# Convolution mixer by token tiles instead of channel halves, and 512-token tiles in the second group's FFN projections

## The reference

```python
def swiglu(x, w_in, w_down):
    a = x @ w_in
    gate, up = jnp.split(a, 2, axis=-1)
    return (jax.nn.silu(gate) * up) @ w_down

def conformer_conv(x, buf, w_in, conv_w, conv_b, ln_g, ln_b, w_out):
    a = x @ w_in                                          # (B, L, 2D)
    glu = a[..., :D_MODEL] * jax.nn.sigmoid(a[..., D_MODEL:])
    ext = jnp.concatenate([buf.astype(glu.dtype), glu], axis=1)   # (B, 30+L, D)
    c = depthwise_conv(ext, conv_w) + conv_b
    c = jax.nn.silu(layernorm(c, ln_g, ln_b))
    return c @ w_out, ext[:, -(CONV_A_WIDTH - 1):]

for i in range(DEPTH):
    f = swiglu(rmsnorm(h, g[0]), ffn_w_in[i, 0], ffn_w_down[i, 0])
    h = h + FFN_HALF * rmsnorm(f, g[1])
    xm = rmsnorm(h, g[2])
    ...                     # mixer i: convolution, gated convolution, gMLP, pooling
    h = h + rmsnorm(m, g[3])
    f = swiglu(rmsnorm(h, g[4]), ffn_w_in[i, 1], ffn_w_down[i, 1])
    h = h + FFN_HALF * rmsnorm(f, g[5])
```

## Time and profile before

| | |
|---|---|
| median of 3 runs | 4662.27 us (4657.13 to 4664.7) |
| the profiled execution | 4654.91 us |
| its span on the slowest core | 4653.4 us |
| spans of the 8 cores | 4644.1 to 4653.4 us |
| TensorE busy | 4566.7 us, 98% |
| VectorE, ScalarE, GpSimd busy | 1770.4, 1281.3, 608.6 us |
| matmuls | 30474 |

### The profile page before, as it was taken

The page is one execution under the profiler, slowest core; times in us unless marked ns, Lnnn a source line. Parts: engine busy times, 40 slices in busy tenths (PEclk is TensorE's granted clock), DMA queues, the critical chain, the costliest instruction groups (busy, mean ns, idle before and its releaser), DMA issues.

```text
span 4653.4 us, 83035 instructions; the slowest of 8 cores (4644.1 to 4653.4 us)
## 1 busy us (share of the span) xinstructions
PE 4566.7 (98%) x30474; PEld 2698.2 (58%) x30474; DVE 1770.4 (38%) x3156; ACT 1281.3 (28%) x2499; POOL 608.6 (13%) x1102
## 2 busy tenths in 40 slices
PE   7998999999999999999999989999999999999999
PEld 4555656556555565565646566565665655656564
DVE  2366232373232542326232472323723236232622
ACT  2135222233221331224121252222322225121421
POOL 1112110011010110102010111101101012010210
PEclk9998999999999999999999999999999999999999
DMA  8336527264263543635565246363543636444361
GB/s 167 68 73 124 103 53 137 48 117 85 55 111 62 106 84 61 118 60 93 98 139 98 63 90 112 57 118 57 105 92 57 117 57 123 73 80 98 60 119 41
DMA packets 228042, 416.39 MB, mean 89 GB/s; under 512 B 114095, under 2 KB 136879, under 8 KB 227630
## 3 DMA queue, kind: packets, MB, share of 16 engines
q0 software_dynamic: 88592, 319.79, 39.6%
q1 hardware_dynamic: 139054, 91.30, 8.0%
HBM read 682.92 MB, written 12.71 MB: 149 GB/s over the span
## 4 chain that ended last, share of the span: by engine, by line
PE 92%; DVE 2%; issue 2%; DMA 2%; SPq 1%; ACT 1%; POOL 0%; DVEq 0%; ACTq 0%; POOLq 0%
PE ps L83 91%; DVE big L88 1%; SPq L242 1%; PE ps L84 1%; ACT big L85 1%; DVE big L86 1%; DMA big<-wst 1%; DMA big<-big 1%; DMA big<-xp 0%; DVE big L89 0%; POOL big L86 0%; DVE big L87 0%; DVEq L167 0%; POOL big L242 0%; ACTq L167 0%
## 5 line engine op out<-in xcount | busy, mean ns | idle before, releaser
L83 PE MATMUL ps<-big 128*128 128x384 bf16 (+5 forms) x29758 | 4535.4, 322 | 47.6 <-DMA big<-big 13.3
L83 PEld LDWEIGHTS ps<-big 128*128 128x128 bf16 (+1 forms) x29758 | 2653.9, 99 | 1897.5 <-issue 137.4
L85 ACT ACTIVATE big<-ps 128x384 f32<-128x384 f32 (+5 forms) x1526 | 875.4, 577 | 2829.1 <-PE ps L83 2721.3
L86 DVE TENSOR_TENSOR big<-ps,big 128x384 bf16<-128x384 f32 (+6 forms) x1386 | 856.6, 618 | 1855.6 <-PE ps L83 1838.0
L88 DVE SCALAR_TENSOR_TENSOR big<-big 128x1024 bf16<-128x1024 f32 (+9 forms) x591 | 585.4, 995 | 184.0 <-POOL big L86 115.8
L242 POOL DMA_DIRECT2D big<-wst x608 | 327.2, 542 | 2456.3 <-PE ps L83 2296.4
L85 ACT ACTIVATE big<-big 128x1024 bf16<-128x1024 f32 (+5 forms) x454 | 344.4, 774 | 480.8 <-DVE big L88 308.7
L86 POOL TENSOR_TENSOR big<-big 128x1 f32<-128x1 f32 (+1 forms) x434 | 261.8, 605 | 1537.7 <-DVE big L87 1313.8
L87 DVE TENSOR_SCALAR big<-big 128x1 f32<-128x1 f32 (+2 forms) x439 | 78.6, 180 | 716.7 <-ACT big L85 703.2
L89 DVE COPY big<-big 32x1136 bf16<-32x1136 bf16 (+4 forms) x281 | 81.7, 291 | 19.5 <-ACT big L85 7.8
L84 PE MATMUL ps<-big 128*128 128x128 bf16 x716 | 57.5, 224 | 29.3 <-DVE big L88 18.1
(11 more groups left out here) (9 smaller groups left out, 20.5 us busy)
## 6 DMA issues: line engine op xcount, KB each, us to landing
big<-wst POOLq DMA_DIRECT2D x608, 512.0 KB, 8.4
big<-gains SPq DMA_DIRECT2D x52, 512.0 KB, 10.6
big<-xp SPq DMA_DIRECT2D x16, 512.0 KB, 5.1
yp<-big SPq DMA_DIRECT2D x16, 512.0 KB, 4.1
big<-big SPq DMA_DIRECT2D x64, 71.0 KB, 2.5
big<-big SPq DMA_DIRECT2D x64, 70.8 KB, 2.7
big<-big SPq DMA_DIRECT2D x48, 64.0 KB, 2.3
big<-dwx SPq DMA_DIRECT2D x4, 512.0 KB, 4.3
```

The costliest lines, as they stand in the source:

```text
L83: 'matmul': lambda e, *a, **k: e.matmul(*a, **k),
L85: 'activation': lambda e, *a, **k: e.activation(*a, **k),
L86: 'tensor_tensor': lambda e, *a, **k: e.tensor_tensor(*a, **k),
```

## The change

Two things change. The convolution mixer projects all eight channel blocks of a token tile before the next token tile, and its passes go by `ct` with both halves together; the slots lent for results are four instead of six, in another order among the weights; the second group has three `xr` buffers instead of two; the DVE copies of a gather are written into DVE's order where its modelled queue is short (`polite`). And in the second group the FFN projections run over two token tiles of 512 instead of 384, 384 and 256; the staging room of 4608 bytes is three buffers of 384 or two of 512, and the class `Widths` keeps overlapping ones apart. The first group's FFNs and the other mixers keep their tiles.

```diff
+class Widths(Pool):
+    CLASH = {0: (3,), 1: (3, 4), 2: (4,), 3: (0, 1), 4: (1, 2)}
...
+    def take(self, wide):
+        c = [i for i in ((3, 4) if wide else (0, 1, 2)) if i not in self.busy and not any(x in self.busy for x in self.CLASH[i])]
+        if not c:
+            return None
+        k = min(c, key=lambda i: self.S.p.rt_w([(self.name, x) for x in (i,) + self.CLASH[i]]))
+        self.S.p.inherit([(self.name, k)], [(self.name, x) for x in self.CLASH[k]])
+        self.busy.add(k)
+        return k
...
                     for q in range(4):
                         cast(('ai', q, 0), ('in', 'a_w_in', q * 256))
                         cast(('ai', q, 1), ('in', 'a_w_in', D + q * 256))
-                        if q == 1:
-                            for i in range(4):
-                                lend(('W', i))
-                            for i in range(2):
-                                lend(('C', i))
-                            lend(('F', 0))
-                            lend(('F', 1))
-                    for i in range(2, 6):
+                    for i in range(2):
+                        lend(('W', 2 * i))
+                        lend(('W', 2 * i + 1))
+                        lend(('C', i))
+                        lend(('F', i))
+                    for i in range(2, 4):
                         lend(('F', i))
...
-        sg = [A.at(SG0 + i * 1536, [384], F32) for i in range(3)]
+        sg = [A.at(SG0 + i * 1536, [384], F32) for i in range(3)] + [A.at(SG0 + i * 2560, [512], F32) for i in range(2)]
...
+        def polite(eng='dve'):
+            while p.efree[eng] > S.now + 0.25:
+                yield p.efree[eng] - 0.15
...
                               lambda kc, t: gb[:, kc, t.sl],
-                              lambda kb, t: [('g', k, t.n, 2 * kb), ('g', k, t.n, 2 * kb + 1)],
+                              lambda kb, t: [('g', k, t.nf, 2 * kb), ('g', k, t.nf, 2 * kb + 1)],
...
+            NX = 2 if smp else 3
...
-                        pr = (k, q // 2, nt.idx, c)
+                        pr = (k, nt.idx, c, 0)
...
-            items = [(ct, 0, None) for ct in range(NCT)] + [(ct, 1, None) for ct in range(NCT)]
+            items = [(ct, hf, None) for ct in range(NCT) for hf in range(2)]
...
-                b = i % 2
+                b = i % NX
...
-                if i >= 2:
-                    yield Flag(('xfree', k, i - 2))
+                if i >= NX:
+                    yield Flag(('xfree', k, i - NX))
...
+                        yield from polite()
                         t2 = p.op('dve', fns, reads=rd, writes=[('xr', b, 'v')], cost=0.9)
...
-                        fkey = 0 if ct == 's' else ct if hf == 0 else 4 + ct % 2
+                        fkey = 0 if ct == 's' else 2 * (ct % 2) + hf
...
+            ntf = nts
+            if g_ > 0:
+                ntf = [NTile(0, 0, 512, 0, taus[0:4]), NTile(1, 512, 512, 0, taus[4:8])]
...
-            ffn_in(k, g_, l, s, nts, gate)
+            ffn_in(k, g_, l, s, ntf, gate)
```

More of the change, by code:

```diff
@@ L354, in give, with __init__ @@
             self.S.push(self.S.now, self.waiters.pop(0))
+class Widths(Pool):
+    CLASH = {0: (3,), 1: (3, 4), 2: (4,), 3: (0, 1), 4: (1, 2)}
+    def __init__(self, S, name):
+        Pool.__init__(self, S, name, 0)
+        self.busy = set()
+    def take(self, wide):
[6 more added lines that the diff above has]
+        return k
+    def give(self, k):
+        self.busy.remove(k)
+        w, self.waiters = self.waiters, []
+        for g in w:
+            self.S.push(self.S.now, g)
 class Banks:
@@ L692, in build_program @@
         exts = A.at(o, [8, 34, 16], BF16); o += 8 * 34 * 16 * 2
-        XR0 = o
-        xr = [A.at(o + i * 16 * NXR * 2, [4, 4, NXR], BF16) for i in range(2)]
-        xrs = [A.at(o + i * 16 * NXR * 2, [4, 2, 512], BF16) for i in range(2)]
-        xrz = [A.at(o + i * 16 * NXR * 2, [8 * NXR], F32) for i in range(2)]
-        o += 2 * 16 * NXR * 2
         glus2 = A.at(o, [8, NS], F32); o += 8 * NS * 4
         glus = A.at(o, [8, NS], F32); o += 8 * NS * 4
-        gluf = A.at(XR0 - 8704, [8, 32], F32)
+        gluf = A.at(o - 1024, [8, 32], F32)
+        XRO = [o, o + 32 * NXR, G0 + 8 * (32 + GP) * 2]
+        assert XRO[2] + 32 * NXR <= o - 1024
+        xr = [A.at(x, [4, 4, NXR], BF16) for x in XRO]
+        xrs = [A.at(x, [4, 2, 512], BF16) for x in XRO]
+        xrz = [A.at(x, [8 * NXR], F32) for x in XRO]
+        o += 2 * 32 * NXR
         assert o <= G0 + GSZ, (o - G0, GSZ)
@@ L721, in build_program @@
         P_XMB = Pool(S, 'xmb', 3)
-        P_SG = Pool(S, 'sg', 3)
+        P_SG = Widths(S, 'sg')
         P_ZB = Pool(S, 'zb', 3)
@@ L730, in grab, with grab_sg @@
             return pool.take()
+        def polite(eng='dve'):
+            while p.efree[eng] > S.now + 0.25:
+                yield p.efree[eng] - 0.15
+        def grab_sg(n):
+            while True:
+                k = P_SG.take(n > 384)
+                if k is not None:
+                    return k
+                yield P_SG
         plan = []
@@ L1007, in ev @@
                 yield p.t(tg)
-                i = yield from grab(P_SG)
+                i = yield from grab_sg(n)
                 ps, pid = bk(bg)
@@ L1071, in ffn_down @@
             yield from tok_mm(k, taus, lambda kc, t: gb[:, kc, t.sl],
-                              lambda kb, t: [('g', k, t.n, 2 * kb), ('g', k, t.n, 2 * kb + 1)],
-                              lambda kb, t: [('g', t.n, 2 * kb), ('g', t.n, 2 * kb + 1)],
+                              lambda kb, t: [('g', k, t.nf, 2 * kb), ('g', k, t.nf, 2 * kb + 1)],
+                              lambda kb, t: [('g', t.nf, 2 * kb), ('g', t.nf, 2 * kb + 1)],
                               [(g_, 'fd', l, s, kb) for kb in range(NQ)], NJ, spawn)
-        XRI = [('xr', i, e) for i in range(2) for e in 'dv']
+        XRI = [('xr', i, e) for i in range(3) for e in 'dv']
         def mixer_a(k, g_, nts, taus, nextlane):
@@ L1091, in init @@
                 p.op('dve', I.memset(glub[:, :, 30 + GP:32 + GP], 0.0), writes=['glub_p'])
-                for i in range(2):
+                for i in range(NX):
                     yield S.now + 1.0
@@ L1259, in conv @@
                     first = ct != 's' or si % 2 == 0
-                    x = i % 2
+                    x = i % NX
                     if ct != 's':
@@ L1273, in conv @@
                             off = None
-                        elif hf == 1 and ct >= 2:
+                        elif ct >= 2:
                             yield Flag(('lnd', k, ct - 2))
-                            p.inherit(ids, [('fb', ct - 2, c) for c in range(4, 8)])
+                            p.inherit(ids, [('fb', ct - 2, c) for c in range(4 * hf, 4 * hf + 4)])
                             off = slot_off(PIDX[(g_, 'F', fkey)])
@@ L1418, in fclose @@
                 yield Flag(('lnd', k, i))
-                lent_close((g_, 'F', i), [('fb', i, c) for c in range(4)])
-                if i >= 2:
-                    lent_close((g_, 'F', 2 + i), [('fb', ct, c) for ct in (i - 2, i) for c in range(4, 8)])
-            for i in range(NCT):
+                for hf in range(2):
+                    lent_close((g_, 'F', 2 * (i % 2) + hf), [('fb', ct, c) for ct in (i - 2, i) for c in range(4 * hf, 4 * hf + 4)])
+            for i in range(2, NCT):
                 S.spawn(fclose(i))
@@ L1449, in ev @@
                 i = yield from grab(P_ZB)
-                i2 = yield from grab(P_SG)
+                i2 = yield from grab_sg(n)
                 zk = zb[i]
@@ L2007, in build_program @@
                    NTile(2, 768, 256, NS if g_ == 0 else 0, taus[6:])]
-            groups.append((taus, nts))
+            ntf = nts
+            if g_ > 0:
+                ntf = [NTile(0, 0, 512, 0, taus[0:4]), NTile(1, 512, 512, 0, taus[4:8])]
+            for n in ntf:
+                for t in n.taus:
+                    t.nf = n.idx
+            groups.append((taus, nts, ntf))
         NSTG = 11
@@ L2020, in start @@
             g_, i = k // NSTG, k % NSTG
-            taus, nts = groups[g_]
+            taus, nts, ntf = groups[g_]
             kind, l, s = KINDS[i]
```

## The result

The changed kernel takes **4609.2 us** (median of 4 runs: 4607.9, 4608.6, 4609.9 and 5199.9), the kernel before 4660.0 beside it: a ratio of 0.9889, 95% interval 0.9871 to 0.9906. Forecast were 4608, inside 4588 to 4642.

What follows compares the result with a forecast made beforehand. TensorE, busy 98% of the span, was taken to bound the kernel. Terms -23.4 + 1 - 21.5 - 10 = -53.9 us, applied to the median of 4662.3, gave 4608 us, range 4588 to 4642.

Steps and rivals of the forecast that it cites:

- FFN tiles: Second group's FFN projections in tiles of 512: a block falls from 7.045 to 6.912 us, over 176 blocks -23.4 us.
- (15 x 48 x 4.5 - 480 x 2.5)/240 = 8.6 ns, a matmul of 115 ns where streaming is 107: Second group's FFN projections: step putting the surplus over streaming on the 256-wide matmuls, 8.6 ns each.
- Wider tile's start: Second group's FFN starts: first tile waits for four token tiles, 0 to 0.5 us in each of seven starts, taken as +1.
- First group's mixer: First group's convolution mixer: by tokens, passes 4 and 5 run under the third tile's projection, fewer gather waits; -21.5 us.
- 10.5 lost: First group's convolution mixer: loss left after the change, 3.5 us small waits, two late landings of 3 us, 1 us low clock.
- Second group's mixer: Second group's convolution mixer: VectorE runs late, but the first norm starts earlier and other work stands as cover; -10 us.
- Of 16 I leave 6: Second group's convolution mixer: of 16 us lost to idle time and low clock, 6 remain after the change.
- covered, with 1.5 us to spare: First group's convolution mixer: the order holds some 16, 16 and 23 us for the gathers of passes 5, 6 and 7.
- rival E: Both convolution mixers: weight pairs hit the gathers of passes 4 to 7, eight hits cost 88 us; slower, 4680; chance 0.06.
- B: Rival: the new convolution order gives nothing back, out-projection waits for weights and clock eat the 31.5 us; 4640; chance 0.15.
- C: Rival: the 256-wide surplus belongs to changing tiles and stays, so the tiles give only -7.6 us; 4624; chance 0.07.
- D: Rival: the last token tile's norms come too late at seven FFN starts, 4.7 us each, 33 us; 4640; chance 0.09.

Runs made afterwards that it cites:

- e8: The changed kernel with the second group's FFN tiles of 256, 512 and 256 tokens; 4655.5 us, ratio 0.9995 to the kernel before.
- e1: The kernel before with only the second group's FFN projections in two 512-token tiles, convolution mixer by channel halves; 4638.0 us, ratio 0.9961.
- e2: The changed kernel without its wide FFN tiles, convolution mixer by tokens in both groups; 4635.1 us, ratio 0.9941 to the kernel before.
- e3: The changed kernel with the second group's convolution mixer put back to channel halves, wide FFN tiles kept; 4618.3 us, ratio 0.9919 to the kernel before.
- e7: The changed kernel without pauses between VectorE's copies for passes 0 to 7, both groups, `polite()` and the older pause removed; 4627.3 us, ratio 0.9937.
- e10: The changed kernel with six weight blocks around the second group's out-projection loading 128 of 2048 columns, instruction order kept; 4602.1 us, ratio 0.9891.
- e4: The changed kernel with the second group's last three in-projection slot pairs given back after pass 5's gather lands in modelled time; 4615.3 us, ratio 0.9905.
- e9: The changed kernel with VectorE's copies for passes 4 and 5 of the second group cut to 32x16 elements, instruction order kept; 4606.6 us, ratio 0.9884.
- e12: The changed kernel with the second group's first out-projection weight block waiting on the chip until pass 4's gather has landed; 4610.6 us, ratio 0.9898.
- e5: The changed kernel with VectorE's copies for passes 4 and 5 of the second group queued at once behind the gather's issue; 4634.2 us, ratio 0.9950.

## Why the prediction was right

The time came out within 2 us, in part by luck. The gain was forecast at 53.9 us and measured as 49.3 in core span (50.5 as the sum of the stretches), so it came out 3 to 5 us too large; the forecast took it off 4662.3, and the kernel before came out at 4660.0 beside the change, which hid 2.3 of that. The terms, too, partly made up for one another.

- **FFN tiles, -23.4: right in size, wrong in cause.** Measured 8 x 2.98 = -23.8, a block at 6.907 us. The size held because it is the difference of two lengths of a block, read or put together from rows, and needs no cause. The step that failed is "(15 x 48 x 4.5 - 480 x 2.5)/240 = 8.6 ns, a matmul of 115 ns where streaming is 107": an average laid over a single wait. The starts of the matmuls show 109 ns at 256, and once in a block a wait of 101 ns for VectorE; e8, with a tile of 512 ahead, makes that wait 236 ns and leaves the 109. Had I gone by the cause that I gave, a 256-wide tile would have looked dear in any order of tiles; it is not its width, but the product of a wide tile just ahead of it. The Trainium skill's formula that I set aside ("TensorE: Matmul & The Clock Gate", Back-to-back issue gap), columns over 2.4 GHz plus 2.5 ns, agrees with the traces at each of these widths: 109 ns at 256, 162.5 at 384, 215.8 at 512. That section of the Trainium skill does not give it for every use, as the prediction has it: it calls it the gap of an isolated matmul, and for a stream of weight loads and matmuls gives about 131 ns at 512; this stream measured 215.8, and the measurement decides. 2816 x 2.5 ns = 7.0 us are the matmuls' share; the other 17 are 176 waits of 0.1 us. The Trainium skill's advice to rotate independent matmuls through PSUM banks ("Perfetto Trace Analysis", Matmuls) names what the old tiling ran into; whether another bank would have saved these waits without wider tiles was not tried.
- **Wider tile's start, +1: wrong sign.** The meeting of the groups and the other mixers give 2.8 - 1.5 = 1.3, 0.3 and 1.7 us beyond the tiles' own price, so about -3 (the first of them within its scatter). In e1 the start did cost 4.24 us once; the new order hides it.
- **First group's mixer, -21.5: a little large.** Measured -18.0 (e2 -15.4, e3 -18.1, with ±2 to 3 between cores). "10.5 lost" was more like 14: idle 12.1 us on the slowest core and a clock of 0.96 over 360:400. The mechanism held: no gather is waited for longer than 2.1 us on the slowest core, since passes 4 and 5 run under the third tile's projection. The pauses between copies have no price in the prediction. Without them some 11 us are lost (e7), but that run also takes out a pause that the kernel before had, so the share of the change's own pause stays open.
- **Second group's mixer, -10: half of it.** Measured -5.2 alone; in the changed kernel -7.3 + 3.0 of the tiles' = -4.3. The step that failed is "Of 16 I leave 6": about 11 are left. I had counted the cover of passes 5 to 7 in the first group ("covered, with 1.5 us to spare"); the second group's term names VectorE alone, and gathers beside weights stand there only in rival E. There the last pieces of pass 4's gather are issued in the same microsecond as the first pair of out-projection weights, and e10 puts 5.0 us on weights beside gathers, clock included; without that the term would be -9.3. VectorE's part, a wait of 2.3 to 3.4 us at pass 5, stayed in e4 and in e9 to e12.

**The rivals.** B (nothing given back) is refuted by e2. C was right that the surplus does not go by width, and wrong that it stays. D happened in e1 and e3 at one start, not in the changed kernel. E's mechanism happened in the second group, mainly at pass 4, for some 5 us in all. In e5, with eight blocks in one crowd, TensorE stood 14.89 us for one gather, so the 6.6 us that E put on each hit were not too high for a crowd, but no run had eight such hits.

**Of what would show it**: a block of 6.91 us, DVE and ACT a little less busy (1745.1 for 1770.4, 1249.7 for 1281.3 us) came true. That no wait for a gather is over 3 us came true on seven of the eight cores (4.04 us on core 1). Idle times of 8 and 5 us were 12.1 and 12.7 on the slowest core (9.1 and 9.4 on core 5), and a 20 us stretch at 0.81 clock was there, in the second group.

## What to carry to other kernels

A mean surplus per instruction is not a price per instruction: look at the starts one by one before saying what it belongs to, since a wait of 0.1 us under a modelled end is listed as busy. Where small gathers and large weight loads share a stretch, ask for each gather which load is issued beside it, pass by pass and group by group; delaying the loads only moves the meeting. Where a planner writes the order, an edit meant for one queue moves all of them, so take the suspected work away in place (shorter copies, smaller loads) to learn what it costs.

## What the runs showed of the hardware

- 256-wide matmuls start 109 ns apart at 1.00 clock, 320-wide ones 135.8, 384-wide ones 162.5 and 512-wide ones 215.8: each has about 2.5 ns on top of its columns at 2.4 GHz.
- A 71 KB transfer within SBUF lands in 2.1 to 3.6 us with no weight load beside it (e4), in 5.9 to 9.0 beside two 512 KB weight loads (changed kernel) and in up to 13.3 beside four (e12). In e5, among eight such loads, one 120 KB transfer of SyncE took 30.7 us. Beside two loads of 32 KB (e10) the gather's pieces land in 2.2 to 3.8 us.
- On core 5 half of what the six small loads gave back (5.3 us there) was not waiting but clock: idle time on core 5 in 2640:2820 fell from 9.4 us to 6.9 (180.00 - 173.13), the granted clock of that stretch rose from 0.97 to 0.99.
